# Stick attention features first, its weight transposes two iterations late, and down-projection rows joined in pairs

## What is computed

```python
# stick attention: 8 heads of 64, 4 blocks of 128 queries
z = einsum('bqhd,bkhd->bhqk', q_blk, k) * scale
mask = key_pos[None, :] < t[:, None]
log_1mb = where(mask, log_sigmoid(-z), 0.0)
suffix = cumsum(log_1mb, axis=3, reverse=True) - log_1mb
att = where(mask, exp(log_sigmoid(z) + suffix), 0.0)
y_att = einsum('bhqk,bkhd->bqhd', att, v)

y = concatenate([rms_norm(y_lru, norm_lru_out), rms_norm(y_att, norm_att_out)], axis=-1)
x = x + einsum('bse,ed->bsd', y, w_out)

# experts, 64 tokens for each of 16
h = einsum('becd,edf->becf', xs, w_gate_up)
hg, hu = split(h, 2, axis=-1)
ye = einsum('becf,efd->becd', silu(hg) * hu, w_down)
```

## Time and profile before

| | us |
|---|---|
| median of 3 runs | 1744.4 (1744.07 to 1746.35) |
| the profiled execution | 1740.37 |
| its span | 1738.2 |
| TensorE busy | 1591.8 (92%) |
| VectorE busy | 729.7 (42%) |
| ScalarE busy | 529.8 (30%) |
| mean granted TensorE clock | 0.961 |

### The profile page before, as it was taken

One profiled execution on the slowest core, in us unless ns is written; L12 is line 12 of the kernel. 1 busy time (PEld: TensorE's weight loads), 2 busy tenths in 40 slices (PEclk: granted clock), 3 DMA queues, 4 the chain that ended last, 5 costly groups with the idle time before them and its releaser, 6 DMA issues.

```text
span 1738.2 us, 20706 instructions
## 1 busy us (share of the span) xinstructions
PE 1591.8 (92%) x7944; PEld 1115.5 (64%) x7944; DVE 729.7 (42%) x1097; ACT 529.8 (30%) x833; POOL 122.8 (7%) x156
## 2 busy tenths in 40 slices
PE   6989799999999998998989989998699999999996
PEld 5667678887887877987667768776333534434332
DVE  4454654434334335384434444355432222321224
ACT  4363434421222223224444433233121213112112
POOL 3000000000000000031101110001600000000002
PEclk9999689999999999999999999999799999999998
DMA  6121022333332323533201212337399999999994
GB/s 214 58 73 57 17 73 73 97 97 97 97 97 89 87 88 118 152 97 98 74 25 54 69 41 73 130 97 312 121 380 416 413 417 415 416 421 415 417 418 183
DMA packets 145095, 307.90 MB, mean 177 GB/s; under 512 B 7328, under 2 KB 98848, under 8 KB 128624
## 3 DMA queue, kind: packets, MB, share of 16 engines
q1 hardware_dynamic: 138992, 294.67, 45.9%
q0 software_dynamic: 3024, 9.10, 1.8%
q10 hardware_dynamic: 2992, 2.91, 0.6%
HBM read 300.36 MB, written 4.56 MB: 175 GB/s over the span
## 4 chain that ended last, share of the span: by engine, by line
PE 77%; DMA 8%; DVE 7%; issue 3%; ACT 3%; ACTq 1%; POOL 0%; SPq 0%; POOLq 0%; DVEq 0%
PE bank L1084 13%; PE bank L1763 11%; PE bank L1765 11%; PE bank L1764 11%; PE bank L1771 4%; PE bank L1772 4%; PE bank L1773 4%; DMA RING<-w_down 3%; DMA RING<-w_gu 3%; PE bank L1810 2%; PE bank L1901 2%; PE bank L1095 2%; PE bank L1039 2%; PE bank L1040 1%; PE bank L1780 1%
## 5 line engine op out<-in xcount | busy, mean ns | idle before, releaser
L1763 PE MATMUL bank<-XH,WH 128*128 128x512 f32 x768 | 305.9, 398 | 9.9 <-DVE WL L1442 4.5
L1764 PE MATMUL bank<-XL,WH 128*128 128x512 f32 x768 | 302.2, 393 | 0.0
L1765 PE MATMUL bank<-XH,WL 128*128 128x512 f32 x768 | 302.1, 393 | 0.0
L1442 DVE TENSOR_TENSOR WL<-RAW,WH 128x2048 fp32r<-128x2048 f32 (+1 forms) x91 | 194.1, 2133 | 155.2 <-ACT WH L1248 155.2
L1084 PE MATMUL bank<-RING,XS 128*64 128x512 f32 x488 | 225.5, 611 | 11.9 <-DMA RING<-w_gu 7.2
L1085 PE MATMUL bank<-RING,XS 128*64 128x512 f32 x496 | 229.1, 611 | 0.0
L1248 ACT ACTIVATE WH<-RAW 128x2048 fp32r<-128x2048 f32 (+1 forms) x91 | 161.8, 1778 | 149.6 <-PE bank L1773 123.5
L1763 PEld LDWEIGHTS bank<-XH,WH 128*128 128x128 f32 x768 | 146.7, 191 | 43.6 <-DVE WL L1442 8.9
L1765 PEld LDWEIGHTS bank<-XH,WL 128*128 128x128 f32 x768 | 146.2, 190 | 31.3
L1764 PEld LDWEIGHTS bank<-XL,WH 128*128 128x128 f32 x768 | 146.5, 191 | 30.0 <-issue 0.2
L1084 PEld LDWEIGHTS bank<-RING,XS 128*64 128x64 f32 x488 | 64.5, 139 | 144.8 <-issue 140.3
(11 more groups left out here) (328 smaller groups left out, 2496.7 us busy)
## 6 DMA issues: line engine op xcount, KB each, us to landing
RING<-w_gu SPq DMA_DIRECT2D x123, 1024.0 KB, 13.5
RING<-w_down SPq DMA_DIRECT2D x64, 1024.0 KB, 11.0
RAW<-w_in SPq DMA_DIRECT2D x66, 512.0 KB, 4.8
RAW<-w_ffn_in SPq DMA_DIRECT2D x44, 512.0 KB, 4.7
RAW<-w_ffn_out SPq DMA_DIRECT2D x20, 512.0 KB, 4.4
RAW<-w_out SPq DMA_DIRECT2D x16, 512.0 KB, 4.5
RAW<-w_branch SPq DMA_DIRECT2D x24, 256.0 KB, 3.0
ONCE<-w_gu SPq DMA_DIRECT2D x5, 1024.0 KB, 16.3
```

Of the source, the lines that this page charges most:

```text
L1442: V.tensor_tensor(WL[:, u % 2, :n], RAW[:, u % 2, :n], WH[:, u % 2, :n].bitcast(F32), ALU.subtract).then_inc(s["w_lo"], 1)
L1763: T.matmul(bank[:, :st.nt], wh[:, k, c], hi, start=k == 0, stop=False)
L1764: T.matmul(bank[:, :st.nt], wh[:, k, c], lo, start=False, stop=False)
L1765: ins = T.matmul(bank[:, :st.nt], wl[:, k, c], hi, start=False, stop=k == st.K - 1)
```

## The change

1. The stick attention's turn becomes S, T(i-2), C(i-2), W, O(i-3), fill.
2. O of the stick attention makes features first (two heads on the 128 partitions, 128 queries along the row), as the grouped one does. ACT squares it to SQ and writes its scaled high part to YAH, DVE the low part to YAL. The sum of squares over features is a product of SQ with a column of ones into a column of PV, one for each O, issued in the next O; the last is in a new step `asum`, which reduces them and makes 1/rms for each token.
3. `rms(YT)` and `tx(YT)` are gone. The eviction of the output projection multiplies by 1/rms of the token (a scalar of the partition) while it adds to X. The LRU's norm is treated in the same way: 16 products with a column of ones, no scaling of YL.
4. The fills come in halves, one in each iteration from 0 to 5 and 10 to 13; memory keys at 6 and 9, norm at 7, split at 8; none from 14 on.
5. Rows 2p and 2p+1 of w_down go to partition p, one run of 8 KB; the transposes of SG take every other feature to match.
6. A sixth ONCE slot (tile 8) at 56 KB; the router's small buffers move to make room, and ACT waits for `icc` before it writes XS over them.

```diff
-    ONCE = {n: at(f"ONCE{n}", kb, [P, 2048]) for n, kb in ((6, 36), (7, 44), (10, 197.5), (11, 181.5), (12, 189.5))}
+    ONCE = {n: at(f"ONCE{n}", kb, [P, 2048]) for n, kb in ((6, 36), (7, 44), (8, 56), (10, 197.5), (11, 181.5), (12, 189.5))}
...
         def o_step(i):
-            mine[i].o = add("O", dict(pv=1, o=1, ohi=int(kind != "stick")), a=mine[i])
-        turn = (((s_step, 0), (w_step, 0), (t_step, 1), (c_step, 1), (o_step, 2), (fill_step, 0)) if kind == "stick" else
+            mine[i].o = add("O", dict(pv=1, o=1, ohi=1, sq=int(kind == "stick")), a=mine[i])
+        turn = (((s_step, 0), (t_step, 2), (c_step, 2), (w_step, 0), (o_step, 3), (fill_step, 0)) if kind == "stick" else
...
-    fill = {0: [lambda: queries(1)], 2: [lambda: keys(1)], 4: [lambda: qkv.append(vals(1))],
-            6: [lambda: add("lsquare", dict(ysq=1), after=qkv[1])], 7: [norm_sum],
-            9: [lambda: add("lsplit", dict(yhi=4, ylo=4), after=qkv[1])], 10: [memk(0)], 12: [memk(1)],
-            14: [lambda: out_half(0, 0)]}
-    last = attention("stick", 4, 4, fill, lambda i: qkv[i // 8])
-    rms(YT, YT, 512, after=last)
-    out_half(1, 0)
-    tx(YT, XH[:, 4:8], XL[:, 4:8], 4, TT, scale=V_GATT, feeds="xa")
+    q1, k1, v1 = (halves(f(1, False)) for f in (queries, keys, vals))
+    fill = {0: [q1[0]], 1: [q1[1]], 2: [k1[0]], 3: [k1[1]], 4: [v1[0]], 5: [lambda: qkv.append(v1[1]())],
+            6: [lambda: add("lsquare", dict(ysq=1), after=qkv[1]), memk(0)], 7: [norm_sum],
+            8: [lambda: add("lsplit", dict(yhi=4, ylo=4), after=qkv[1])], 9: [memk(1)],
+            **{10 + 2 * j + h: [f] for j in range(2) for h, f in enumerate(out_half(j, 0, in_two, first=2))}}
+    stick_last = attention("stick", 4, 4, fill, lambda i: qkv[i // 8])
+    add("asum", dict(ass=1, asq=1, arc=1, rat=1), after=stick_last)
     for j in range(2):
         out_half(j, 1)
...
-    dn_v = w_down[0].rearrange("e (i k p) d -> p (e i) k d", k=2, p=P)
+    dn_v = w_down[0].rearrange("e (i p k) d -> p (e i) (k d)", k=2, p=P)
...
+                    if first:
+                        act.wait_ge(s["icc"], 1)
...
-                        ins = T.transpose(HB[:, CAP * f:CAP * f + CAP], SG[:, f * P:f * P + P], ident[0:CAP, 0:CAP])
+                        c = slice(f // 2 * 2 * P + f % 2, f // 2 * 2 * P + 2 * P, 2)
+                        ins = T.transpose(HB[:, CAP * f:CAP * f + CAP], SG[:, c], ident[0:CAP, 0:CAP])
...
+            elif k == "O" and st.a.att == "stick":
+                src, hi, _ = features(st.a)
+                act.wait_ge(s["pv"], st.a.n + 1)
+                A(SQ[:, :], src, ACT.Square).then_inc(s["sq"], 1)
+                A(hi, src, ACT.Copy, scale=vec(V_GATT + st.a.h)).then_inc(s["ohi"], 1)
...
+                    if "part" in st.kw:
+                        dve.wait_ge(s["rat" if st.kw["part"] else "lrs"], 1)
+                        c = 32 + 4 * st.kw["part"] + r
+                        V.scalar_tensor_tensor(xs, shaped(st, bank), ST[:, c:c + 1], xs, ALU.mult,
+                                               ALU.add).then_inc(s["evD"], 1)
+                        continue
...
+            if st.src == "ya":
+                wait(pe, "o", stick_last.end)
...
+        def square_sum(a):
+            c = 256 + 4 * a.h + a.qt[0]
+            pe.wait_ge(s["sq"], a.n + 1)
+            return T.matmul(PV[:, c:c + 1], SQ[:, :], ones[:, 0:1], start=True, stop=True)
...
-                for c in range(4):
-                    ins = T.matmul(LIN[lin_of[st.r0]][:, :], ones, YSQ[:, c, :], start=c == 0, stop=c == 3)
+                for t in range(TT):
+                    for c in range(4):
+                        ins = T.matmul(LIN[lin_of[st.r0]][:, t:t + 1], YSQ[:, c, t * P:t * P + P], ones[:, 0:1],
+                                       start=c == 0, stop=c == 3)
...
-                for kt in range(a.nkt[0] if a.att != "stick" else 0):
+                for kt in range(a.nkt[0]):
...
-                for j in range(2 if a.att == "stick" else 0):
-                    for kt in range(a.nkt[j]):
-                        ins = T.matmul(PV[:, j * P:j * P + 64], PT[:, kt, j * P:j * P + P], values(a, j, kt),
-                                       start=kt == 0, stop=kt == a.nkt[j] - 1)
+                if a.att == "stick" and a.n:
+                    ins = square_sum(atts[a.n - 1])
```

More of the change, by code:

```diff
@@ L209, in build @@
                lexp lgl lt lm2 lsq lin lrec ysq yn yhi ylo qk mx e_ab msk p tr ptA ptD pv o rope rxn rope_p
-               ms_hi ms_lo saved band0 band1 x2h x2l xal lgp lgs afp af top ixp icc rcp pn ohi t1A t1D wrp xt_ps xtA xtD lgc lg2 fms fsd fnr ftn fnrm""".split()
+               ms_hi ms_lo saved band0 band1 x2h x2l xal lgp lgs afp af top ixp icc rcp pn ohi t1A t1D wrp xt_ps xtA xtD lgc lg2 sq ass rat lrs asq arc fms fsd fnr ftn fnrm""".split()
     names.extend(["rms_q", "rsd_q"])
@@ L264, in unit, with in_two @@
         take_banks(st)
-        st.now = (0,) if split else range(nres)
+        st.now = range(split or nres)
         return st
     def rest(st):
-        more = add("rest", dict(res=1, evA=int(st.who[1] == "act"), evD=int(st.who[1] == "dve")), a=st)
-        more.now = (1,)
+        now = range(len(st.now), len(st.who))
+        sh = [st.who[r] for r in now]
+        more = add("rest", dict(res=len(sh), evA=sh.count("act"), evD=sh.count("dve")), a=st)
+        more.now = now
         return more
-    def in_two(*args, **kw):
+    def in_two(*args, first=1, **kw):
         made = []
-        return [lambda: made.append(unit(*args, split=True, **kw)), lambda: rest(made[0])]
+        return [lambda: made.append(unit(*args, split=first, **kw)), lambda: rest(made[0])]
     def take_banks(st):
@@ L375, in build, with made, queries, keys @@
     add("lgate", dict(gmm=8, sig=8), after=lgu)
[L377 to L384, removed]
+    def made(args, kw, now):
+        return unit(*args, **kw) if now else (args, kw)
+    def queries(j, now=True):
+        return made((win, 1024 + UC * j, KT, "F", "scaled"), dict(dst=lambda r: QT[:, 2 * j + r, :], scale=0.125), now)
+    def keys(j, now=True):
+        return made((win, 1536 + UC * j, KT, "F", "copy"), dict(dst=lambda r: KTT[:, 2 * j + r, :]), now)
+    def vals(j, now=True):
+        return made((win, 2048 + UC * j, KT, "T", "copy"),
+                    dict(dst=lambda r: VT[:, 2 * r:2 * r + 2, UC * j:UC * j + UC]), now)
     qkv = []
@@ L605, in features @@
     def features(a):
+        if a.att == "stick":
+            q = slice(a.qt[0] * P, a.qt[0] * P + P)
+            return PV[:, 0:P], YAH[:, a.h, q], YAL[:, a.h, q]
         hi, lo = (YH3, YL3) if a.att == "gqa" else (YH2, YL2)
@@ L692, in load @@
                 row = (QE * p + 2 * i + (c - 16) // 4) * 4 + c % 4
-                src = dn_v[:, bass.ds(row, 1), :, :].rearrange("p a k d -> p (a k) d")
-                sp.dma_start(slot.rearrange("p (k d) -> p k d", k=2), src).then_inc(landed, 16)
+                src = dn_v[:, bass.ds(row, 1), :].rearrange("p a f -> p (a f)")
+                sp.dma_start(slot, src).then_inc(landed, 16)
         def body(p, first, last):
@@ L1384, in _ @@
                 act.wait_ge(s["res"], st.r0 + 1)
-                A(RBC[:, :], LIN[lin_of[st.r0]][:, :], ACT.Sqrt, scale=1.0 / 512, bias=eps6).then_inc(s["evA"], 1)
+                A(ST[:, 32:36], LIN[lin_of[st.r0]][:, 0:TT], ACT.Sqrt, scale=1.0 / 512, bias=eps6).then_inc(s["evA"], 1)
                 act.preload_act_table_set("sigmoid_and_others")
             elif k == "lsplit":
-                act.wait_ge(s["yn"], 1)
+                wait(act, "res", st.after.end)
                 for c in range(4):
@@ L1416, in _ @@
                 ins.then_inc(s["ptA"], 1)
-            elif k == "O" and st.a.att != "stick":
+            elif k == "asum":
+                act.wait_ge(s["asq"], 1)
+                A(ST[:, 36:40], ST[:, 124:128], ACT.Sqrt, scale=1.0 / 512, bias=eps6).then_inc(s["arc"], 1)
+            elif k == "O" and st.a.att == "stick":
[3 more added lines that the diff above has]
+                A(hi, src, ACT.Copy, scale=vec(V_GATT + st.a.h)).then_inc(s["ohi"], 1)
+            elif k == "O":
                 src, hi, _ = features(st.a)
@@ L1685, in _ @@
                 wait(dve, "evA", st.end)
-                link(V.reciprocal(RBC[:, :], RBC[:, :]))
-                V.tensor_tensor(YL_[:, :, :], YL_[:, :, :], RBC[:, :].unsqueeze(1).to_broadcast([P, 4, S]),
-                                ALU.mult).then_inc(s["yn"], 1)
+                V.reciprocal(ST[:, 32:36], ST[:, 32:36]).then_inc(s["lrs"], 1)
+            elif k == "asum":
+                dve.wait_ge(s["ass"], 1)
+                V.tensor_reduce(ST[:, 124:128], PV[:, 256:272].rearrange("p (h t) -> p t h", h=4), AX,
+                                ALU.add).then_inc(s["asq"], 1)
+                dve.wait_ge(s["arc"], 1)
+                V.reciprocal(ST[:, 36:40], ST[:, 36:40]).then_inc(s["rat"], 1)
             elif k == "lsplit":
-                dve.wait_ge(s["yn"], 1)
```

63 lines of the change are left out of this document (31 added, 32 removed).

## The result

| | before | changed |
|---|---|---|
| median | 1744.2 (1744.07 to 1746.35, 4 runs) | 1722.9 (1721.83 to 1727.42, 4 runs) |
| profiled execution | 1740.4 | 1721.9 |
| its span | 1738.2 | 1720.1 |
| mean granted TensorE clock | 0.961 | 0.966 |

The ratio is 0.988 with the interval [0.986, 0.990]: 21.4 us off the median. The forecast was 1719, with 1706 to 1730 around it. Faster is right, and the measured median lies in the range, 3.9 us above the forecast.

A forecast was written before the change was run, and what follows sets the result against it. Stick attention was taken as TensorE-bound with holes paid twice (idle, then slow clock), the experts as DMA-bound. Savings of 21.5 and 3.9 us, 25.4 off the median, gave 1719 us, range 1706 to 1730.

The forecast's parts named there:

- The place of the gain: Stick attention 21.5 us less, PB waits gone, 16 value records in 1.02 us; expert stage 3.9 us less.
- The sum of work: Stick attention: TensorE work of 130.0 us at 2.4 GHz, including square sums of 3.4 us at 0.107 a record.
- Iterations 0 to 6 run without a hole: Stick attention: half fills of 5.5 us cover W and the splits, so TensorE does not wait in these iterations.
- Rival (b): Stick attention: longer chains or ACT's steps make covered iterations wait, half a microsecond on 16 iterations; 1727 us, chance 0.15.
- The middle: Stick attention, iterations 7 and 8 without a product: 3.3 us idle, plus 5 us lost to a 1.2 GHz clock.
- The tail: Stick attention after fill 13, nothing covering: 16.7 us with 7.7 of work, 9.0 idle; 4.4 of work twice as long.
- the product behind it: Output projection after the tail: wide products of 11.0 us each; out_half(0,1) starts at slow clock, included in +2.3 us.
- The experts: Expert stage: joined w_down rows move at 422 instead of 411 GB/s, 59 tiles by 0.066 us, 3.9 us less.
- The early slot, ACT's wait and the strided loads: Expert-stage side effects: sixth early tile slot, ACT's wait for icc, SG's strided loads; each taken as 0 us.
- (c): Rival, expert stage: the join does nothing and w_down stays at 411 GB/s; 1723 us, chance 0.09.
- (a): Rival, stick attention: the clock holds 2.4 GHz through middle and tail, 11.7 us less; 1707 us, chance 0.12.
- (d): Rival, stick attention: 1.2 GHz from iteration 7 to the tail's end, +44 us; 1763 us, chance 0.04.

The follow-up runs named there:

- e3: The changed kernel, but products writing to bank 1 no longer wait for the sigmoids of the scores; median 1717.9 us, ratio 0.984.
- the square: Four kernels with the changed features-first form: transposes one or two iterations late, fills whole or in halves; medians 1729.7, 1725.4 (whole), 1717.9, 1724.0 us (halves).
- e1: The kernel before with only w_down's joined rows and SG's matching strided columns; median 1741.2 us, ratio 0.999.
- e2: The changed kernel without the sixth early slot (ONCE slot 8) for an expert weight tile; median 1723.6 us, ratio 0.989.
- e0: The changed kernel itself, run again with no edit; median 1724.0 us, ratio 0.988 to the kernel before.
- e12: The changed kernel with transposes one iteration late, no sigmoid wait in bank 1, and the LRU's split ahead of W8; median 1711.0 us, ratio 0.982.
- e10: The changed kernel with transposes one iteration late instead of two, fills still in halves; median 1717.9 us, ratio 0.985.
- e8: The changed kernel with the LRU's split moved to iteration 6 and the second memory-key product to 8; median 1719.9 us, ratio 0.988.
- e14: The changed kernel with transposes one iteration late and whole fills instead of halves; median 1729.7 us, ratio 0.993.
- e4: The changed kernel with the second memory-key product in iteration 8, ahead of the LRU's split; median 1722.9 us, ratio 0.988.

## Why the prediction was right, and where it was off

**The place of the gain: right.** In the profiled pair, whose spans differ by 18.1 us, the stick attention takes 18.2 less, the experts 3.8 less, and the rest 3.9 more. The waits for PB went, the values run at 0.064 a record as taken. Chain of the changed kernel, the norm, the values and a square sum:
```profile
183.87 3.59 PE bank L1917 x32
...
214.62 1.02 PE bank L1954 x16
215.65 0.31 PE bank L1843 x2
```
**The sum of work, about -0.5.** Of the rows here the square sum is the one to look at. It was taken at 0.107 a record, from L1920 with its 64 columns, as the upper end. The chain gives the pair 0.31, but then the first product behind it has only 0.34, where a first product without a square sum before it has 0.43. The timeline's starts are the plainer measure:
```profile
215.57 0.38 PE L1843 MATMUL bank<-CST,SQ 128*128 128x1 f32 x2
215.82 0.48 PE L1798 MATMUL bank<-WH,XH 128*128 128x512 f32 x1
```
That is 0.25 for two records, 0.12 each, 3.9 for 32 of them against 3.4. The bound was passed by a little: nothing of one column had been seen, and fewer columns were taken to cost no more. The norm, 32 such records in a row, took 3.59, or 0.112 each.

**"Iterations 0 to 6 run without a hole": wrong, -3.6.** This is the step that failed, though the total came out in the range. The forecast followed the chain of W, the split and PV, and left out what a fill itself waits for: its bank. The three rows of waits for SE above are 3.6 us, from fills in iterations 1, 5, 12 and 13. e3 shows their worth: 4.1 us in the stretches where they stood, 2.1 of the stage. The row of before (L1763, 1.1 us) could have told of them. Rival (b), which let covered iterations wait, had the right place, but another cause and more than twice the size (8 us).

**The middle, -0.7: right in size, half right in cause.** Forecast were 3.3 us idle and 5 lost to the clock, 8.3. In 183.87 to 207.80 TensorE is idle for 2.1, and the clock of 0.71 says that 58% of 23.9 us, 13.9, ran at 1.2 GHz, so that about 7 were lost: 9.0. That W8 holds up DVE's queue was foreseen; that the queue's customer would be the LRU's split, and behind it a whole product, was not: the forecast named the split of O5. It also put the low clock down to a hole. That each slow stretch begins after idle time is so in the kernel before, but in the changed one the clock falls at 188 to 189 us and the hole opens only at 193 (last section).

**The tail, +1.9.** Forecast were 16.7 us and 4.4 for the clock, 21.1; measured 19.2. For the product behind it, 22.0 + 2.3 against 24.65: right, -0.3. What the forecast did not ask is whether the tail is needed. It costed the lag of two with its cover and found none missing; it did not cost the lag of one with halves, which the square shows to be 7 us better.

These make -0.5 - 3.6 - 0.7 + 1.9 - 0.3 = -3.2, against the 3.3 between 21.5 and 18.2. That it closes so well is luck in part: the tail's own square sums stand in two of the terms, and the stage has a noise of 1 us.

**The experts: right.** 59 tiles by 0.066 us, 3.9, against 3.8 measured and 3.6 in e1 alone. Thirteen profiled executions with the join have 457.3 to 460.0 us between the marks, with a median of 457.7, against 461.5 in the one without it. By the rule of the Trainium skill on descriptors ("DMA: Bandwidth & Descriptors", "Why small descriptors are slow"), a fixed cost for each packet, it would by an estimate have been 1.8, by its "Specifications", full rate from 512 B on, none; the trace agrees with neither. The early slot, ACT's wait and the strided loads: 0, as taken; e2 shows it for the slot alone, e1 for the loads together with the join, and ACT's wait was not run by itself.

**The rivals.** The total says little between them. (c), the join without effect, was priced at 1723, which is where the median came out; only the queues' rows and e1 refute it. (a) is refuted by the clock in middle and tail. (d) would need 25 us of added slow time; windows of 5 us are at 1.00 throughout iterations 0 to 6 and 10 to 13.

**The rest of the distance is the clock elsewhere.** In the pair of profiled executions the span came out 7.3 us above the forecast 1712.8: 3.3 from the stage, 0.1 from the experts and 3.9 from the rest, nearly all of it (3.6) between the end of the stage and the last rounding of weights, in code that the change does not touch. Between equal marks, identical code differs there by 0.5 to 2.6 us, in either direction. One such place, before first, then changed:
```profile
400.00:405.00 5.00, 3.15 (x14) 2.67 (x15) 3.20 (x4) 2.43 (x2) 0.00 (x0) 1.00 0.00 0
```
```profile
382.00:387.00 5.00, 3.28 (x8) 2.67 (x9) 3.15 (x3) 2.43 (x2) 0.00 (x0) 0.66 0.02 3
```
Both windows hold the larger part of the same hole of 2.3 us. In the kernel before the clock stays; in the changed one it falls, and the stretch to the next mark takes 13.7 us instead of 12.2. e0, the same code once more, has 12.3 there, yet 1.6 more in each of three other places behind the stage; so these dips are not tied to places of the code. Most of e3's 4 us are of this kind: between three pairs of marks it is 0.6, 1.6 and 1.6 us shorter than e0. But the five runs of e3 (1714.2 to 1719.3) and of e0 (1722.3 to 1725.4) do not overlap, so this is more than scatter from one execution to the next; with one profile of each, what ties it to e3 is not shown. So a median may shift by some microseconds in stretches that no edit touches, and e12's 6.8 against e10's, with 2.1 in the stage, should not be read as the worth of its two edits. Why a given hole drops the clock in one execution and not in the next stays open; no run was made for it.

## What to carry to other kernels

Follow a moved piece of work to everything it waits for, its output bank too: a wait that was covered by the first half of a unit is bare once the unit starts with it. Where two edits cover the same hole (a longer lag, smaller fills), cost each alone and both together, and look at what the longer pipeline does to its uncovered end. And where several rivals give the same total, name beforehand the row that parts them.

## What was not expected of the hardware

**The clock falls with TensorE busy.** In e3, windows of 5 us around the norm:
```profile
175.00:180.00 5.00, 5.00 (x43) 4.75 (x43) 3.54 (x6) 3.73 (x5) 0.00 (x0) 1.00 0.00 0
180.00:185.00 5.00, 5.00 (x48) 4.66 (x47) 2.83 (x10) 2.79 (x7) 0.00 (x0) 0.89 0.65 206
185.00:190.00 5.00, 5.00 (x21) 3.15 (x23) 0.48 (x3) 2.97 (x5) 0.00 (x0) 0.50 0.02 7
```
TensorE is busy for all of the 15 us, and still the clock goes to 0.50. What it does there is the norm, from 181.61 on, 32 records of one column each (timeline of e3):
```profile
181.61 4.87 PE L1917 MATMUL bank<-CST,YSQ 128*128 128x1 f32 x32
```
The changed kernel shows the same, there with the fall just behind its norm:
```profile
183.00:188.00 5.00, 5.00 (x49) 4.48 (x44) 2.30 (x9) 2.81 (x6) 0.00 (x0) 1.00 0.68 210
188.00:193.00 5.00, 5.00 (x28) 2.86 (x24) 2.83 (x5) 4.80 (x10) 0.00 (x0) 0.58 0.01 3
```
The same norm took 3.6 us in the changed kernel, 4.7 in e3, 5.1 in e8 and e14 and 5.2 in e4, but also 5.1 in e0, whose code is the changed kernel's; so its time does not belong to an edit. No run kept the old form of the norm, so whether its one-column records or the small operations ahead of them bring the clock down is open.

**A product of one column is not cheap.** 0.112 us a record in a row of 32, and 0.12 from start to start as a pair between other operations. With a load of 128 x 128 weights for each record, that is near the 0.107 of L1920 with 64 columns; with a load half as wide, 128 columns took 0.064. Between these rows the cost went with the load and not with the columns; no run changed one of the two alone.
